# The second block's attention: last turned copy and output scaling on VectorE, scores between the transposes

## The chip, the cores and the metric

The kernel runs on one core of one Trainium2 chip. The metric is the device time of one execution in microseconds (us); the profile is one further execution of the same program, taken by the hardware profiler. TensorE (PE) multiplies matrices and transposes tiles, its weight loads (PEld) run ahead of its matmuls; VectorE (DVE), ScalarE (ACT) and GpSimd (POOL) work elementwise; SyncE (SP) issues DMAs. Each engine runs its own list of instructions in order, and the lists meet at semaphores only.

## What is computed

The reference is a long chain: a first block (latent attention, mLSTM, mixture of experts) and a second block of two layers. The change touches the attention of the second block alone, which is run once in each layer (l = 0 and l = 1). Cut to that:

```python
# k_all, v_all: 256 context tokens and then 1024 latent tokens; 4 query heads of 64, 2 key/value heads
def latent_attention(q, k_all, v_all):          # 1024 queries, 1280 keys
    s = einsum('bqhd,bkhd->bhqk', q, k_all)     # float32 scores, in blocks of 128 queries
    return einsum('bhqk,bkhd->bqhd', softmax(s), v_all)
# layer 0 also attends the 256 context queries to the 256 context keys; layer 1, the last, does not
o_att = silu(z) * attention                     # one of four branches of the layer
```

## The kernel before

The program is a row of phases with a barrier of all engines after each. In each layer of the second block they are: norm, `project_in`, `attention_2`, `fourier`, `project_out`. Nothing of the next phase's engine work begins before `attention_2` has ended; the weights of the later phases are fetched by DMA during it (`prefetch`, early in SyncE's list).

`attention_2` walks a list `items` of tiles, a tile being 128 queries of one head. Long tiles have 1280 keys, short tiles (context queries, layer 0 only) have 256. Layer 0 has, for each of 4 heads, 8 long tiles and then 2 short ones, 40 in all; layer 1 has 4 times 8 long tiles, 32 in all. For tile n the work is:

- `scores(n)`, TensorE: queries times keys into the PSUM tile `at_sc` (two buffers of three banks), with the key split into a high and a low part `kh`, `klo`: six matmuls for 1280 keys, two for 256.
- `maximum(n)`, VectorE: the row maximum, and with it the bias of the exponential.
- `exp(n)`, ScalarE: the exponential into `at_p` (two buffers), with its row sum in `total`; `inv` is the reciprocal, taken on VectorE.
- `turn`, TensorE: the 128x128 pieces of `at_p` are transposed into the PSUM tile `at_tb`, which has two buffers of one bank. The pieces go in groups of four: a long tile has the groups g0 and g1 of four pieces and g2 of two; a short tile has one group of two.
- copy of each turned group from `at_tb` to `at_pT`: on ScalarE (`copy_turned`).
- `output(n)`, TensorE: `at_pT` times `at_v`, 10 matmuls (20 records) for a long tile, written into the free part of the bank in which the last group of tile n+1 lies, right after that group's transposes.
- scaling of the output by `inv` and copy out of PSUM (`copy_output`): on ScalarE, after the copy of that last group.

TensorE's list for tile n: first `scores(n + 2)`, then g0, g1, g2, then `output(n - 1)`. Uses of the two `at_tb` buffers are numbered; `full` says that TensorE has filled a use, `free` that it has been read out. Before the last group, TensorE waits for these:

```python
                            m = first_use[n] - 1
                            pe.wait_ge(free[m % 2], m // 2 + 1)
                            if first_use[n] - first_use[n - 1] > 1:
                                pe.wait_ge(free[1 - m % 2], (m - 1) // 2 + 1)
```

that is, all groups of tile n - 1 have been copied; the group itself also needs its own buffer, which g0 of the same tile held. ScalarE's list for tile n: `exp(n + 1)`, copy g0, copy g1, copy g2, scale the output of tile n - 1. VectorE's: `maximum(n + 1)`, reciprocal of tile n.

Once in each call, before head 2, the keys are exchanged (`KEYS_1`): ScalarE makes `kh` anew (`split_high`) when all scores of heads 0 and 1 are done, VectorE then makes `klo`, and only then may `scores` of the first tile of head 2 go. In ScalarE's list this stands ahead of the tile `2 * per_head - 2`, behind everything of the tile before it.

In the profile the line of a matmul made by the helper `accumulate` is L145 (scores and outputs alike; the tile names tell them apart), that of a transpose L3091, the copies are L3173, the scaled output L3168, the exponential L3151, the maximum L3210 and L3213.

Of the kernel before, what the change touches and what calls it, by code (L numbers as in the profile page):

```python
# [11 lines left out]
ALU = mybir.AluOpType  # L12
ACT = mybir.ActivationFunctionType
# [3 lines left out]
P = 128  # L17
# [31 lines left out]
H2, KVH, HD = 4, 2, 64  # L49
# [2937 lines left out]
def attention_2(nc, g, l, last, prefetch):  # L2987
# [5 lines left out]
    with Phase(nc, f"at{l}") as ph:  # L2993
# [4 lines left out]
        p = ph.sb("p", [P, 2, N_ALL])  # L2998
        pT = ph.sb("pT", [P, 2, NT, P])
# [5 lines left out]
        full = [ph.sem(f"full{b}") for b in range(2)]  # L3005
        free = [ph.sem(f"free{b}") for b in range(2)]
        names = ("scored", "maxed", "bias_ready", "exped", "inv_ready", "raw_in", "high", "low", "y_done",
                 "cleared", "y_turned", "pool_high", "pool_low", "first_in")
        scored, maxed, bias_ready, exped, inv_ready, raw_in, high, low, y_done, cleared, y_turned, pool_high, pool_low, first_in = (
            ph.sem(n) for n in names)  # L3010

        items = []
# [36 lines left out]
        def half(h):  # L3049

            return slice((h % 2) * HD, (h % 2) * HD + HD)

        with nc.Block() as block:
# [30 lines left out]
            @block.tensor  # L3084
            def _(pe):
                def turn(n, srcs, more=None):
                    b = n % 2
                    if n >= 2:
                        pe.wait_ge(free[b], n // 2)
                    for k, src in enumerate(srcs):  # L3090
                        mm = pe.transpose(tb[:, b, k * P:(k + 1) * P], src, g.ident[:])  # L3091
                    if more is not None:
                        mm = output(b, more)
                    mm.then_inc(full[b], 1)

                def output(b, n):
                    h, _, keys = items[n]
                    return accumulate(nc, tb[:, b, 2 * P:2 * P + HD], [
                        (pT[:, n % 2, k, :], v[:, k, (h // 2) * HD:(h // 2 + 1) * HD]) for k in range(keys // P)])

                def scores(n):
                    h, q0, keys = items[n]
                    if n == 0:
                        pe.wait_ge(cleared, 1)
                    if n % per_head == 0:
                        pe.wait_ge(*need[h])
                        if h == 2:
                            split_done(pe, KEYS_1)
                    if n >= 2:
                        pe.wait_ge(exped, n - 1)  # L3110
                    for c0 in range(0, keys, BANK):
                        cols = slice(c0, min(c0 + BANK, keys))
                        mm = accumulate(nc, sc[:, n % 2, c0 // BANK, 0:cols.stop - c0], [
                            (q[:, h % 2, q0:q0 + P], kh[:, cols]), (q[:, h % 2, q0:q0 + P], klo[:, cols])])
                    mm.then_inc(scored, 1)

                for c, (t0, tn) in enumerate(groups(N_ALL)):
                    turn(c, [g.parts[:, V_AT, (t0 + k) * P:(t0 + k + 1) * P] for k in range(tn)])
                scores(0)
                scores(1)  # L3120
                for n, (h, q0, keys) in enumerate(items):
                    if n + 2 < len(items):
                        scores(n + 2)
                    pe.wait_ge(exped, n + 1)
                    gs = groups(keys)
                    for c, (t0, tn) in enumerate(gs):

                        more = n - 1 if c == len(gs) - 1 and n else None
                        if more is not None:
                            m = first_use[n] - 1  # L3130
# [3 lines that stand above are left out]
                        turn(first_use[n] + c, [p[:, n % 2, (t0 + k) * P:(t0 + k + 1) * P] for k in range(tn)], more)  # L3134
                end = first_use[-1]
                for m in (end - 1, end - 2):
                    pe.wait_ge(free[m % 2], m // 2 + 1)
                output(end % 2, len(items) - 1).then_inc(full[end % 2], 1)
                pe.wait_ge(y_done, 1)
                for n, (t, c0, cn) in enumerate(ends):  # L3140
                    for c in range(cn):
                        mm = pe.transpose(sc[:, n // 3, n % 3, c * P:(c + 1) * P],
                                          y[t][:, c0 + c, :], g.ident[:])
                    mm.then_inc(y_turned, 1)

            @block.scalar
            def _(act):
                def exp(n):
                    h, q0, keys = items[n]
                    act.wait_ge(bias_ready, n + 1)  # L3150
                    act.activation(p[:, n % 2, 0:keys], sc[:, n % 2].rearrange("p b n -> p (b n)")[:, 0:keys], ACT.Exp,  # L3151
                                   bias=st[:, n % 2, 1:2], scale=g.rq[:, q0 // P, h:h + 1],
                                   accum_out=total[:, n % 4:n % 4 + 1]).then_inc(exped, 1)

                def split_high(i):
                    what, h = loads[i]
                    loaded(act, i)
                    if i == KEYS_1:
                        act.wait_ge(scored, 2 * per_head)
                    if what == "k":  # L3160
                        act.activation(kh[:], raw[:], ACT.Copy).then_inc(high, 1)
                    else:
                        act.activation(q[:, h % 2, lo:], source(i)[:, lo:], ACT.Copy).then_inc(high, 1)

                def copy_output(b, n):
                    h, q0, _ = items[n]
                    act.wait_ge(inv_ready, n + 1)
                    return act.activation(y[h // 2][:, q0 // P, half(h)], tb[:, b, 2 * P:2 * P + HD], ACT.Copy,  # L3168
                                          scale=inv[:, n % 4:n % 4 + 1])

                def copy_turned(m, dst, w, output_of=None):
                    act.wait_ge(full[m % 2], m // 2 + 1)
                    ins = act.activation(dst, tb[:, m % 2, 0:w], ACT.Copy)  # L3173
                    if output_of is not None:
                        ins = copy_output(m % 2, output_of)
                    ins.then_inc(free[m % 2], 1)

                split_high(KEYS_0)
                split_high(QUERIES_0)
                for c, (t0, tn) in enumerate(groups(N_ALL)):  # L3180
                    copy_turned(c, v[:, t0:t0 + tn, :].rearrange("p t d -> p (t d)"), tn * P)
                exp(0)
                for n in range(len(items)):
                    if n in splits_at:
                        split_high(splits_at[n])
                    if n + 1 < len(items):
                        exp(n + 1)
                    gs = groups(items[n][2])
                    for c, (t0, tn) in enumerate(gs):
                        copy_turned(first_use[n] + c, pT[:, n % 2, t0:t0 + tn, :].rearrange("p t d -> p (t d)"), tn * P,  # L3190
                                    n - 1 if c == len(gs) - 1 and n else None)
                end = first_use[-1]
                act.wait_ge(full[end % 2], end // 2 + 1)
                copy_output(end % 2, len(items) - 1).then_inc(y_done, 1)

            @block.vector
            def _(dve):
# [9 lines left out]
                def maximum(n):  # L3207
# [5 lines left out]
                    dve.tensor_scalar(st[:, n % 2, 1:2], st[:, n % 2, 0:1], g.rq[:, q0 // P, h:h + 1], -1.0,  # L3213
                                      ALU.mult, ALU.mult).then_inc(bias_ready, 1)

                split_low(KEYS_0)
                split_low(QUERIES_0)
                maximum(0)
                for n, (h, q0, keys) in enumerate(items):
                    if n in splits_at:  # L3220
                        split_low(splits_at[n])
                    if n + 1 < len(items):
                        maximum(n + 1)
                    dve.wait_ge(exped, n + 1)
                    dve.reciprocal(inv[:, n % 4:n % 4 + 1], total[:, n % 4:n % 4 + 1]).then_inc(inv_ready, 1)
                for n, (t, c0, cn) in enumerate(ends):
                    dve.wait_ge(y_turned, n + 1)
                    cols = slice(c0 * P, (c0 + cn) * P)
                    dve.tensor_tensor(g.o[2 + t][:, cols], sc[:, n // 3, n % 3, 0:cn * P], g.parts[:, ZA_AT + t, cols], ALU.mult)
# [457 lines left out]
```

## Time and profile before

| | |
|---|---|
| runs | 3838.62 us median of 3 (3837.56 to 3839.77) |
| the profiled execution | 3839.44 us, its span 3837.7 us |
| busy over the span | TensorE 3337.1 us (87%), VectorE 1843.9 (48%), ScalarE 1473.2 (38%), GpSimd 709.8 (18%) |
| attention of layer 0 | about 2818 to 3012 us of the span; TensorE busy 164.7 of 194.0 |
| attention of layer 1 | about 3512 to 3699 us of the span; TensorE busy 161.9 of 187.0 |

The two attentions are a tenth of the time. Shares of busy time over the whole span say little about them; they have to be read from their own stretches, and there from the waits of the engine that is busiest.

### The profile page before, as it was taken

Reading aid. Unit: us, or ns where it says so; the run is one execution under the profiler, and the core shown is the slowest. Engines: PE = TensorE matmul, PEld = TensorE weight load, DVE = VectorE, ACT = ScalarE, POOL = GpSimd, SP = SyncE. Lnnn points to the kernel's source line nnn. Section 1 sums busy time; section 2 is a strip of 40 time slices with the busy share of each in tenths; the row PEclk is TensorE's granted clock in tenths of the full one; section 3 lists DMA queues with packets and bytes.
Section 4 is the critical chain, followed back from the end, with each engine's and each line's share of the span. In section 5 each row is a group of like instructions: output and inputs, shape, how many; then the busy total and the mean of one; then the engine's idle time right before and its main releaser. Section 6 shows DMA issues by size and latency. Waiting matters only on the chain. (4 is left out here: it accounts for less than half of the span.)

```text
span 3837.7 us, 42815 instructions
## 1 busy us (share of the span) xinstructions
PE 3337.1 (87%) x17015; PEld 2690.6 (70%) x17015; DVE 1843.9 (48%) x2343; ACT 1473.2 (38%) x2230; POOL 709.8 (18%) x463
## 2 busy tenths in 40 slices
PE   6999998999999499794999996399978895998889
PEld 3777775777777377573878875288867684886767
DVE  3366874334333354646888885614323433252333
ACT  4222322333434144433777774421145304113531
POOL 2100100000110144202555543400000002000000
PEclk7999999999999699896999998599999997999989
DMA  5335554001010121327999995311030023113002
GB/s 185 110 102 180 187 185 134 24 24 31 24 41 1 57 108 54 138 94 293 382 381 380 389 380 184 132 48 37 27 110 8 23 88 107 53 46 100 13 11 89
DMA packets 235384, 475.87 MB, mean 124 GB/s; under 512 B 25539, under 2 KB 120644, under 8 KB 235188
## 3 DMA queue, kind: packets, MB, share of 16 engines
q1 hardware_dynamic: 219600, 415.26, 31.2%
q0 software_dynamic: 15264, 57.70, 4.5%
q8 instruction: 140, 2.29, 0.2%
q14 instruction: 56, 0.46, 0.0%
q10 hardware_dynamic: 324, 0.15, 0.0%
HBM read 410.50 MB, written 55.22 MB: 121 GB/s over the span
## 5 line engine op out<-in xcount | busy, mean ns | idle before, releaser
L2371 DVE TENSOR_TENSOR exp_wl<-wts_raw,exp_wh 128x2048 fp32r<-128x2048 f32 x144 | 393.9, 2770 | 105.9 <-ACT exp_wh L2331 105.9
L2331 ACT ACTIVATE exp_wh<-wts_raw 128x2048 fp32r<-128x2048 f32 x192 | 368.0, 1919 | 196.0 <-PE exp_gate L2260 64.1
L2704 PE MATMUL pr_ps<-l_h_high,pr_wh 128*128 128x512 f32 (+1 forms) x896 | 335.4, 374 | 18.9 <-DVE pr_wl L2843 18.9
L2705 PE MATMUL pr_ps<-l_h_low,pr_wh 128*128 128x512 f32 (+1 forms) x896 | 330.5, 369 | 0.0
L2706 PE MATMUL pr_ps<-l_h_high,pr_wl 128*128 128x512 f32 (+1 forms) x896 | 329.8, 368 | 0.0
L729 PE MATMUL in_ps<-iw_h_high,in_wh 128*128 128x512 f32 (+1 forms) x696 | 274.9, 395 | 13.9 <-DVE in_wl L907 13.9
L2229 POOL TENSOR_TENSOR exp_wl<-wts_raw,exp_wh 128x2048 fp32r<-128x2048 f32 x48 | 228.9, 4770 | 263.5 <-ACT exp_wh L2331 263.5
L730 PE MATMUL in_ps<-iw_h_low,in_wh 128*128 128x512 f32 (+1 forms) x696 | 264.6, 380 | 0.0
L731 PE MATMUL in_ps<-iw_h_high,in_wl 128*128 128x512 f32 (+1 forms) x696 | 264.1, 379 | 0.0
L2843 DVE TENSOR_TENSOR pr_wl<-pw_raw,pr_wh 128x512 fp32r<-128x512 f32 x88 | 60.1, 691 | 357.8 <-ACT pr_wh L2765 356.0
L2704 PEld LDWEIGHTS pr_ps<-l_h_high,pr_wh 128*128 128x128 f32 x896 | 170.2, 190 | 50.5 <-DVE pr_wl L2843 19.7
L1305 DVE TENSOR_REDUCE att_st<-att_sc 128x1 f32<-128x1280 f32 x64 | 95.4, 1491 | 213.6 <-PE att_sc L145 213.4
L3210 DVE TENSOR_REDUCE at_st<-at_sc 128x1 f32<-128x1280 f32 (+1 forms) x72 | 98.8, 1372 | 200.9 <-PE at_sc L145 200.9
L2705 PEld LDWEIGHTS pr_ps<-l_h_low,pr_wh 128*128 128x128 f32 x896 | 170.1, 190 | 30.2 <-issue 2.4
L2706 PEld LDWEIGHTS pr_ps<-l_h_high,pr_wl 128*128 128x128 f32 x896 | 169.8, 190 | 28.3
L729 PEld LDWEIGHTS in_ps<-iw_h_high,in_wh 128*128 128x128 f32 x696 | 133.2, 191 | 50.3 <-DVE in_wl L907 14.3
L2765 ACT ACTIVATE pr_wh<-pw_raw 128x512 fp32r<-128x512 f32 x88 | 54.9, 630 | 275.0 <-PE pr_ps L2706 268.5
L145 PE MATMUL at_tb<-at_v,at_pT 128*128 128x64 f32 x1312 | 157.4, 275 | 1.4 <-ACT at_y L3168 1.4
L145 PEld LDWEIGHTS at_tb<-at_v,at_pT 128*128 128x128 f32 x1312 | 155.2, 195 | 1.6 <-ACT at_y L3168 1.6
L3173 ACT ACTIVATE at_pT<-at_tb 128x512 f32<-128x512 f32 (+1 forms) x200 | 97.6, 526 | 152.4 <-PE at_tb L145 149.4
L145 PE MATMUL att_tb<-att_pT,att_v 128*128 128x128 f32 x1280 | 153.5, 275 | 0.7 <-ACT att_pT L1272 0.7
L730 PEld LDWEIGHTS in_ps<-iw_h_low,in_wh 128*128 128x128 f32 x696 | 133.1, 191 | 28.9 <-issue 5.1
(505 smaller groups left out, 7559.4 us busy)
## 6 DMA issues: line engine op xcount, KB each, us to landing
wts_raw<-in_w_e_gate SPq DMA_DIRECT2D x64, 1024.0 KB, 9.8
wts_raw<-in_w_e_up SPq DMA_DIRECT2D x64, 1024.0 KB, 9.3
wts_raw<-in_w_e_down SPq DMA_DIRECT2D x64, 1024.0 KB, 7.7
in_mw<-in_w_mod SPq DMA_DIRECT2D x80, 512.0 KB, 4.5
pw_raw<-in_w_in SPq DMA_DIRECT2D x88, 256.0 KB, 2.9
iw_raw<-in_w_in SPq DMA_DIRECT2D x74, 256.0 KB, 4.7
mod_w<-in_w_mod SPq DMA_DIRECT2D x4, 2048.0 KB, 11.9
wo_w<-in_w_out SPq DMA_DIRECT2D x2, 4096.0 KB
```

Source lines behind the costliest of these rows:

```text
L145: mm = nc.tensor.matmul(out, lhsT, rhs, start=n == 0, stop=n == last)
L729: nc.tensor.matmul(out, wh[:, slot, k, :], hi, start=h == 0 and k == 0, stop=False)
L730: nc.tensor.matmul(out, wh[:, slot, k, :], lw, start=False, stop=False)
L731: mm = nc.tensor.matmul(out, wl[:, slot, k, :], hi, start=False, stop=h == 1 and k == KH - 1)
L2229: pool.tensor_tensor(wl[:, POOL_SLOT], raw[:, m % RAW_RING], wh[:, POOL_SLOT].bitcast(F32), ALU.subtract).then_inc(low_pool, 1)
L2331: act.activation(wh[:, m % RING], raw[:, m % RAW_RING], ACT.Copy).then_inc(high, 1)
L2371: dve.tensor_tensor(wl[:, m % RING], raw[:, m % RAW_RING], wh[:, m % RING].bitcast(F32), ALU.subtract).then_inc(low, 1)
L2704: nc.tensor.matmul(out, wh[:, slot, k, :], hi, start=h == 0 and k == 0, stop=False)
L2705: nc.tensor.matmul(out, wh[:, slot, k, :], lw, start=False, stop=False)
L2706: mm = nc.tensor.matmul(out, wl[:, slot, k, :], hi, start=False, stop=h == 1 and k == KH - 1)
L3173: ins = act.activation(dst, tb[:, m % 2, 0:w], ACT.Copy)
L3210: dve.tensor_reduce(st[:, n % 2, 0:1], sc[:, n % 2].rearrange("p b n -> p (b n)")[:, 0:keys], AX.X, ALU.max).then_inc(maxed, 1)
```

## The change

VectorE takes over the copy of each tile's last turned group and the scaling of the output (`copy_last`, `copy_output`), one step later in its own list; ScalarE keeps the exponentials and the copies of the other groups. Since ScalarE's list no longer meets TensorE's at the end of a tile, `exp(n)`, which overwrites `p`, gets a wait of its own: a new semaphore `p_turned` counts the tiles whose last group has been transposed. And on TensorE `scores(n + 2)` moves from ahead of tile n's transposes to between its g0 and g1 (in a short tile, which has one group, it stays where it was).

```diff
@@ TensorE
                     for k, src in enumerate(srcs):
                         mm = pe.transpose(tb[:, b, k * P:(k + 1) * P], src, g.ident[:])
                     if more is not None:
+                        mm.then_inc(p_turned, 1)
                         mm = output(b, more)
                     mm.then_inc(full[b], 1)
...
                 for n, (h, q0, keys) in enumerate(items):
-                    if n + 2 < len(items):
-                        scores(n + 2)
                     pe.wait_ge(exped, n + 1)
                     gs = groups(keys)
                     for c, (t0, tn) in enumerate(gs):
 
+                        if c == min(1, len(gs) - 1) and n + 2 < len(items):
+                            scores(n + 2)
                         more = n - 1 if c == len(gs) - 1 and n else None
@@ ScalarE
                 def exp(n):
                     h, q0, keys = items[n]
                     act.wait_ge(bias_ready, n + 1)
+                    if n == 2:
+                        m = first_use[1] - 1
+                        act.wait_ge(full[m % 2], m // 2 + 1)
+                    if n > 2:
+                        act.wait_ge(p_turned, n - 2)
...
-                    gs = groups(items[n][2])
-                    for c, (t0, tn) in enumerate(gs):
-                        copy_turned(first_use[n] + c, pT[:, n % 2, t0:t0 + tn, :].rearrange("p t d -> p (t d)"), tn * P,
-                                    n - 1 if c == len(gs) - 1 and n else None)
-                end = first_use[-1]
-                act.wait_ge(full[end % 2], end // 2 + 1)
-                copy_output(end % 2, len(items) - 1).then_inc(y_done, 1)
+                    for c, (t0, tn) in enumerate(groups(items[n][2])[:-1]):
+                        copy_turned(first_use[n] + c, pT[:, n % 2, t0:t0 + tn, :].rearrange("p t d -> p (t d)"), tn * P)
@@ VectorE
+                def copy_output(b, n):
+                    h, q0, _ = items[n]
+                    dve.wait_ge(inv_ready, n + 1)
+                    return dve.tensor_scalar(y[h // 2][:, q0 // P, half(h)], tb[:, b, 2 * P:2 * P + HD], inv[:, n % 4:n % 4 + 1],
+                                             None, ALU.mult)
+
+                def copy_last(n):
+                    t0, tn = groups(items[n][2])[-1]
+                    m = first_use[n + 1] - 1
+                    dve.wait_ge(full[m % 2], m // 2 + 1)
+                    ins = dve.tensor_copy(pT[:, n % 2, t0:t0 + tn, :].rearrange("p t d -> p (t d)"), tb[:, m % 2, 0:tn * P])
+                    if n:
+                        ins = copy_output(m % 2, n - 1)
+                    ins.then_inc(free[m % 2], 1)
...
                     dve.wait_ge(exped, n + 1)
                     dve.reciprocal(inv[:, n % 4:n % 4 + 1], total[:, n % 4:n % 4 + 1]).then_inc(inv_ready, 1)
+                    if n:
+                        copy_last(n - 1)
+                copy_last(len(items) - 1)
+                end = first_use[-1]
+                dve.wait_ge(full[end % 2], end // 2 + 1)
+                copy_output(end % 2, len(items) - 1).then_inc(y_done, 1)
```

TensorE's list in layer 0's attention, one tile and the beginning of the next, among the long tiles of head 0 (`at_sc` the scores, `at_tb` transposes of `at_p` and the output). Before:

```order
L3091 MATMUL at_tb<-g_ident,at_p 128x128 x10
L145 MATMUL at_tb<-at_v,at_pT 128x64 x10
L145 MATMUL at_sc<-at_kh,at_q 128x512
L145 MATMUL at_sc<-at_klo,at_q 128x512
L145 MATMUL at_sc<-at_kh,at_q 128x512
L145 MATMUL at_sc<-at_klo,at_q 128x512
L145 MATMUL at_sc<-at_kh,at_q 128x256
L145 MATMUL at_sc<-at_klo,at_q 128x256
```

and with the change, at the same place:

```order
L3091 MATMUL at_tb<-g_ident,at_p 128x128 x6
L145 MATMUL at_tb<-at_v,at_pT 128x64 x10
L3091 MATMUL at_tb<-g_ident,at_p 128x128 x4
L145 MATMUL at_sc<-at_kh,at_q 128x512
L145 MATMUL at_sc<-at_klo,at_q 128x512
L145 MATMUL at_sc<-at_kh,at_q 128x512
L145 MATMUL at_sc<-at_klo,at_q 128x512
L145 MATMUL at_sc<-at_kh,at_q 128x256
L145 MATMUL at_sc<-at_klo,at_q 128x256
```

Four of a tile's ten transposes now go ahead of the scores; nothing is added or taken away. ScalarE's list at the same tiles, before:

```order
L3173 ACTIVATE at_pT<-at_tb 128x512 x2
L3173 ACTIVATE at_pT<-at_tb 128x256
L3168 ACTIVATE l_parts<-at_tb,at_inv 128x64
L3151 ACTIVATE at_p,at_total<-at_sc,at_st,l_rq 128x1280
```

and VectorE's list for one tile with the change, where the last two rows are new:

```order
L3202 TENSOR_REDUCE at_st<-at_sc 128x1
L3205 TENSOR_SCALAR at_st<-at_st,l_rq 128x1
L3232 RECIPROCAL at_inv<-at_total 128x1
L3218 COPY at_pT<-at_tb 128x256
L3211 TENSOR_SCALAR l_parts<-at_tb,at_inv 128x64
```

ScalarE's second and third rows have become VectorE's fourth and fifth, and stand there behind the maximum of tile n + 1 and the reciprocal of tile n.

## Rows read from the trace of the kernel before

**Rows 1.** Waits of the weight loads (PEld), attention of layer 0: total, times, longest

```profile
PEld at_tb L3091 <- issue: 28.8, 33, 1.5
PEld at_sc L145 <- issue: 4.3, 2, 3.5
PEld at_sc L145 <- ACT at_p L3151: 2.7, 4, 1.5
PEld at_tb L145 <- ACT at_y L3168: 0.8, 1, 0.8
...
PEld at_sc L3142 <- ACT at_y L3168: 0.5, 1, 0.5
```

**Rows 2.** The same, attention of layer 1

```profile
PEld at_tb L3091 <- issue: 23.5, 31, 1.5
...
PEld at_sc L145 <- issue: 4.1, 2, 3.5
PEld at_sc L145 <- ACT at_p L3151: 2.4, 1, 2.4
...
PEld at_tb L3091 <- ACT at_y L3168: 0.7, 2, 0.5
...
PEld at_tb L3091 <- ACT at_pT L3173: 0.4, 1, 0.4
```

**Rows 3.** Timeline, one long tile, layer 0: start, duration, instruction [idle before, releaser]

```profile
2843.61 1.43 ACT L3151 ACTIVATE at_p<-at_sc,at_st,l_rq 128x1280 f32<-128x1280 f32 x1
...
2844.05 0.90 PEld L3091 LDWEIGHTS at_tb<-g_ident,at_p 128*128 128x128 f32 x8
...
2845.00 1.09 ACT L3173 ACTIVATE at_pT<-at_tb 128x512 f32<-128x512 f32 x2
2845.72 0.20 PEld L3091 LDWEIGHTS at_tb<-g_ident,at_p 128*128 128x128 f32 x2 [0.77 <-issue]
...
2848.38 0.39 ACT L3173 ACTIVATE at_pT<-at_tb 128x256 f32<-128x256 f32 x1 [2.29 <-PE at_tb L145]
...
2848.86 1.42 ACT L3151 ACTIVATE at_p<-at_sc,at_st,l_rq 128x1280 f32<-128x1280 f32 x1
```

**Rows 4.** Timeline, a tile without a stall of TensorE, and the way to an exponential

```profile
2864.19 0.24 PEld L3091 LDWEIGHTS at_tb<-g_ident,at_p 128*128 128x128 f32 x2
...
2866.63 0.19 PEld L145 LDWEIGHTS at_sc<-at_kh,at_q 128*128 128x128 f32 x1
...
2867.80 0.24 PEld L3091 LDWEIGHTS at_tb<-g_ident,at_p 128*128 128x128 f32 x2
...
2868.10 1.49 DVE L3210 TENSOR_REDUCE at_st<-at_sc 128x1 f32<-128x1280 f32 x1 [1.80 <-PE at_sc L145]
...
2869.62 0.22 DVE L3213 TENSOR_SCALAR at_st<-at_st,l_rq 128x1 f32<-128x1 f32 x1
...
2869.88 1.42 ACT L3151 ACTIVATE at_p<-at_sc,at_st,l_rq 128x1280 f32<-128x1280 f32 x1 [0.53 <-DVE at_st L3213]
```

**Rows 5.** VectorE's nearest operations out of PSUM: count | busy us, mean ns | idle before

```profile
L2551 DVE TENSOR_SCALAR l_parts<-fin_tp,fin_gain,g_mod 128x128 f32<-128x128 f32 x40 | 13.6, 402 | 6.8 <-PE fin_tp L2594 6.8
...
L2887 DVE TENSOR_SCALAR l_parts<-pr_ex 128x256 f32<-128x256 f32 x2 | 0.8, 424 | 0.3 <-PE pr_ex L145 0.2
```

**Rows 6.** Timeline, the exchange of keys in layer 1

```profile
3592.57 1.27 ACT L3161 ACTIVATE at_kh<-at_raw 128x1280 fp32r<-128x1280 f32 x1
...
3595.45 0.76 PE L145 MATMUL at_sc<-at_kh,at_q 128*128 128x512 f32 x1 [3.40 <-issue]
...
3602.86 0.47 PE L145 MATMUL at_sc<-at_kh,at_q 128*128 128x512 f32 x1
```

**Rows 7.** Busy time by stretch, layer 1: PE, PEld, DVE, ACT, POOL, PEclk, DMA share, GB/s

```profile
3575.00:3580.00 5.00, 4.43 (x36) 4.05 (x35) 1.77 (x3) 2.96 (x6) 0.00 (x0) 1.00 0.00 0
...
3595.00:3600.00 5.00, 4.55 (x16) 3.89 (x17) 3.81 (x7) 2.44 (x4) 0.00 (x0) 0.50 0.52 108
...
3685.00:3690.00 5.00, 5.00 (x33) 4.57 (x32) 0.00 (x0) 1.78 (x4) 0.00 (x0) 0.68 0.01 3
```

More of the change, by code:

```diff
@@ L3007, in attention_2 @@
         names = ("scored", "maxed", "bias_ready", "exped", "inv_ready", "raw_in", "high", "low", "y_done",
-                 "cleared", "y_turned", "pool_high", "pool_low", "first_in")
-        scored, maxed, bias_ready, exped, inv_ready, raw_in, high, low, y_done, cleared, y_turned, pool_high, pool_low, first_in = (
+                 "cleared", "y_turned", "pool_high", "pool_low", "first_in", "p_turned")
+        scored, maxed, bias_ready, exped, inv_ready, raw_in, high, low, y_done, cleared, y_turned, pool_high, pool_low, first_in, p_turned = (
             ph.sem(n) for n in names)
@@ L3163, in split_high, with copy_turned @@
                         act.activation(q[:, h % 2, lo:], source(i)[:, lo:], ACT.Copy).then_inc(high, 1)
[L3165 to L3171, printed above, removed]
+                def copy_turned(m, dst, w):
                     act.wait_ge(full[m % 2], m // 2 + 1)
[L3173 to L3176, printed above, removed]
+                    act.activation(dst, tb[:, m % 2, 0:w], ACT.Copy).then_inc(free[m % 2], 1)
                 split_high(KEYS_0)
```

## The prediction

> **What bounds the kernel now.** The change lies in two phases of their own, so I read those alone and ask who sets a tile's length. TensorE does: it is busy for 85 to 87% of them (the table above). I take its weight loads (PEld) as its clock, since their start times run without overlap. In layer 0 they wait 28.8 + 4.3 + 2.7 us, and 3.3 in five small rows (0.8 to 0.5) [rows 1], 39.1 in all; in layer 1 23.5 + 4.1 + 2.4, and 2.5 in four small rows (0.8, as the largest small one of layer 0, to 0.4) [rows 2], 32.5. Together 71.6 us: more than this change can't take from the waits.
>
> Where the largest of them comes from is seen in one tile [rows 3]. TensorE loads for its first eight transposes from 2844.05 to 2844.95. The two turned groups could be copied then, but ScalarE began `exp(n + 1)` only at 2843.61 and copies from 2845.00; g2 needs g0's buffer, so TensorE's next load stands 0.77 us. Why is the exponential late? Its scores were long done. ScalarE stood 2.29 us, until TensorE had ended `output(n - 1)`, then copied g2 (2848.38) and scaled the output, and only then could the next exponential start (2848.86). So it is a ring: output, copy of g2 and scaling, exponential, copy of g0, g2's transposes. A tile takes 2848.86 - 2843.61 = 5.25 us.
>
> A short tile without such a stall gives TensorE's own work: from 2864.19 to 2867.80, that is 3.61 us for two transposes, an output and scores [rows 4], of which the scores are 1.17. With 0.90 for the eight transposes [rows 3] a long tile is 4.51 us of work. The stall costs 5.25 - 4.51 = 0.74.
>
> The second wait is 3.5 us at the exchange of keys, once in each layer [rows 1, 2]: ScalarE turns to `kh` only after scaling an output (3592.57), VectorE's half follows, and TensorE goes on at 3595.45 after 3.40 us of nothing [rows 6]. Behind it the granted clock is 0.50 in its stretch against 1.00 in the ordinary tiles [rows 7], which is the 1.2 GHz level: that tile takes 3602.86 - 3595.45 = 7.41 us instead of 4.51.
>
> **The change, part by part.** Nothing is added on TensorE but a signal. I set t = 0 at the first load of tile n's g0 and walk one long tile in the new order: g0 to 0.45, `scores(n + 2)` to 1.62, g1 to 2.07, g2 to 2.30, output to 4.5. A signal of TensorE reaches its waiter 0.30 after the last load here (2867.80 to 2868.10) [rows 4]; for transposes and outputs I take 0.2 to 0.25.
>
> *VectorE's pair.* The trace has no such copy. A read of the same 128x256 from PSUM took 0.42 [rows 5]. For the scaling, 128x64, the bounds are nothing and the 0.40 of a 128x128 with two scalars [rows 5]; taking the slope of one column per ns between these two rows it comes nearer 0.3, and I use 0.28. The pair is then 0.70 (at most 0.42 + 0.40, or, were the copy as dear as both, 1.1). On ScalarE both took 0.48 until it was free again [rows 3]. The Trainium skill (VectorE: DVE Perf Modes, The TRN2 errata) gives 120 cycles plus one a column at 0.96 GHz for VectorE out of PSUM. That would be 0.39 and 0.19, 0.58 for the pair, and the sum below would be 1 to 2 us larger; it also says that ScalarE sits closer to PSUM, which no row here shows for these shapes.
>
> VectorE waits for `full` of tile n - 1, which comes at t = 0.25, and is done by 1.0. First to need it is g1 (its bank), at 1.62: 0.6 us of cover, so the pair may cost 1.3 before a long tile feels it. Behind the waiting copy in VectorE's list stands `maximum(n + 2)`, whose scores are there at 1.9: not delayed.
>
> *ScalarE.* Maximum 1.49, 1.52 to the next step, 0.26 from there to the exponential (2869.62 to 2869.88) [rows 4]. `exp(n + 1)` so starts at 1.62 - 4.53 + 0.30 + 1.52 + 0.26 = -0.83; its copies follow 1.39 later (2843.61 to 2845.00) [rows 3], at 0.56, and g0 is full at 0.64. Its copy of about 0.6 ends near 1.3; g2 wants it at 2.07. The new wait for `p_turned` (t = 2.5 of the tile before) lies ahead of the exponential's bias (3.7 on the same scale) and costs nothing. So the ring is open and a long tile is TensorE's own 4.5 us. Both halves of the change are needed for it. In the old order g2 would follow g0's end by 0.45, g1's transposes alone, while signal and copy take 0.9: with ScalarE free 0.45 of stall would stay. The scores put 1.17 more between them. By the walk described next, the copies alone gain 27 us, the new order alone loses 1, and both gain 46.
>
> *What is left.* I walked all 40 and 32 tiles with these durations. The same walk in the old order gives 71.2 us of waits (the rows 71.6). In the new order it leaves, in layer 0: the wait for the first exponential 2.5 and for the last output 0.6, as before; 1.4 until the ring is running; 0.3 in tiles 7 and 8 of each head, where short scores cover less of VectorE's pair (2.5); 0.57 and 0.87 in the first long tile after the short ones, three times (4.3); 1.0 before each of the last outputs, for VectorE's pair, which was 0.7 on ScalarE (3.0); 0.2 and at the exchange of keys 1.1. Together 15.6. In layer 1: 2.5, 0.6, 1.4, exchange 0.6 + 1.3 + 0.9, last tiles 2.1: 9.4. The gain is 71.2 - 25.0 = 46.2; I take 46.
>
> *The exchange of keys* is in this sum. ScalarE's list reaches `kh` right after copying g1, 2.8 us into the tile before, not behind its output: done 4.1, VectorE's half (as long as a maximum) 5.6, while the new order wants the scores at 4.5 + 0.45. About 0.6 of the 3.4 stays. With no idle of 3.4 us in front, the slow clock behind it should stay away: 7.41 - 4.51 = 2.9 us in layer 1 [rows 6, 4, 3]; in layer 0 a short tile stands there, half the work, for which I estimate 1.5. Together 4.4.
>
> Sum: 46 + 4.4 = 50.4 us. From the profiled execution, 3839.44, that gives 3789.0; it was 0.8 above the median, so I predict 3788 us. No DMA hides it: SyncE's fetches for later phases are issued early in the phase, and its end is a barrier.
>
> **The rivals.** *One, the forecast (80 in 100)*: 40 to 62 us less. The near end is the pair at 1.1 (the walk gives 17.5 + 22.4 + 4.4 = 44) and some cost of going from transposes to scores and back, which no row has; at 0.1 a tile 6 us more is lost. The far end has half of the waits that the walk leaves, (25.0 - 6.2) / 2 = 9 us more, and 3 for less of the slow clock in the last tiles, which by [rows 7] come at 0.68.
>
> *Two, half (10 in 100)*: TensorE pays for the interleaving 0.2 to 0.4 us a tile, 64 tiles, 13 to 26 us: 3801 to 3814. The trace shows no gap when output turns to scores or scores to transposes, one after another in every tile [rows 4]; that speaks against it.
>
> *Three, the clock (4 in 100)*: TensorE's clock falls in stretches without long scores. In the last tiles, which have none, the granted clock was 0.68 with TensorE wholly busy [rows 7]. If the same came at the short tiles of each head, at 2.9 us each time as behind the keys, four times cost 12 and the first keys' gain goes: about 3802. Against it: there are short scores between, and the mix over a tile is what it was while idle time shrinks. The Trainium skill (TensorE: Matmul & The Clock Gate, Part 4) says that transposes do not count as activity for the clock. Were that what decides, the new order, which parts scores and outputs by transposes on both sides, could lose the full clock in every long tile; the trace has 1.00 in tiles with ten transposes in a row [rows 7].
>
> *Four, slower (3 in 100)*: VectorE's pair becomes the ring. Past 1.3 us each microsecond of it lengthens the long tile by as much; at 1.3 + 0.74 = 2.05 nothing is gained, and at 3 us 64 tiles lose 0.95 each, 61 us, less the 4 of the clock: about 3895. The rows put the pair at a third of the point where it decides.
>
> *Five, nothing (3 in 100)*: something else of the phase (an exponential waiting for `p_turned`, VectorE's list in disorder) takes the place of the stall, within 0.2% of before, about 8 us, which is what a measurement of this kernel can tell.
>
> **How the numbers follow.** The likeliest case gives 3788. The range takes it whole and the nearer part of the second and third: 3776 to 3804. Faster by over 0.2%: 0.94; within: 0.03; slower: 0.03.
>
> **What would show it.** In the changed profile: long tiles 4.5 us apart; no wait of g2 for ScalarE's copy; VectorE's COPY 128x256 near 0.42 and its TENSOR_SCALAR 128x64 near 0.28; ScalarE waiting for `at_tb` transposes and no longer for outputs; a wait of under 1.5 us at the keys and a clock of 1.00 behind it; the phases, by the stretches of the table, near 169 and 160 us long. I am wrong if TensorE waits for VectorE in ordinary long tiles, if its own work in a tile is over 4.7 us, or if the clock falls in new places.

## The result and the profile after

The changed kernel took 3782.93 us (median of 4 runs, 3778.48 to 3788.15) against 3839.19 before: ratio 0.9845, 95% interval 0.9823 to 0.9867, 56 us less. The forecast was 3788, with 3776 to 3804. On another chip it took 3786.61 (ratio 0.9856, 0.9835 to 0.9877). Its profiled execution took 3785.64 us, its span 3783.6.

To see where the time went I cut every span at the same points: in either layer the first scores and the first of the transposes that close the attention's phase (L3142 before, L3143 after, L3144 where reads were added). The starts are read from TensorE's timeline of each run, in us. The experiments, which are told below, stand in the same table; `rest` is what follows layer 1's phase, and `long tile` is the distance of one long tile from the next:

| run | before layer 0's scores | phase, layer 0 | between | phase, layer 1 | rest | long tile |
|---|---|---|---|---|---|---|
| before | 2818.7 | 192.6 | 502.4 | 183.1 | 140.9 | 5.25 |
| changed | 2815.9 | 166.0 | 502.7 | 156.1 | 142.9 | 4.44 |
| changed, again | 2819.3 | 165.8 | 500.0 | 156.3 | 142.5 | 4.44 |
| e1_order | 2817.1 | 195.9 | 502.4 | 187.6 | 139.3 | 5.25 |
| e2_copies | 2817.6 | 178.4 | 501.1 | 167.4 | 141.3 | 5.02 |
| e3_extra1 | 2818.6 | 170.7 | 500.4 | 159.7 | 140.4 | 4.44 |
| e4_extra3 | 2821.4 | 191.5 | 501.2 | 167.9 | 141.1 | 4.76 |
| e5_keys | 2816.3 | 164.9 | 500.9 | 151.6 | 140.4 | 4.44 |
| e6_both | 2819.2 | 163.6 | 501.5 | 151.0 | 141.2 | 4.44 |
| e7_extra6 | 2818.0 | 243.7 | 500.6 | 203.6 | 142.7 | 5.75 |

The two phases give 26.6 + 27.0 = 53.6 us. The stretches that the change doesn't touch differ by up to 5.5 us from run to run, so the phases are the better measure of a part.

One long tile of the changed kernel in its timeline, the counterpart of [rows 3]:

```profile
2842.36 1.42 ACT L3157 ACTIVATE at_p<-at_sc,at_st,l_rq 128x1280 f32<-128x1280 f32 x1 [0.74 <-DVE at_st L3205]
2843.11 0.48 PEld L3091 LDWEIGHTS at_tb<-g_ident,at_p 128*128 128x128 f32 x4
...
2843.42 0.42 DVE L3218 COPY at_pT<-at_tb 128x256 f32<-128x256 f32 x1 [1.03 <-PE at_tb L145]
...
2843.77 0.27 DVE L3211 TENSOR_SCALAR l_parts<-at_tb,at_inv 128x64 f32<-128x64 f32 x1
2843.87 0.60 ACT L3173 ACTIVATE at_pT<-at_tb 128x512 f32<-128x512 f32 x1
...
2844.73 0.68 PEld L3091 LDWEIGHTS at_tb<-g_ident,at_p 128*128 128x128 f32 x6
2845.03 1.49 DVE L3202 TENSOR_REDUCE at_st<-at_sc 128x1 f32<-128x1280 f32 x1 [0.99 <-PE at_sc L145]
2845.38 2.31 PEld L145 LDWEIGHTS at_tb<-at_v,at_pT 128*128 128x128 f32 x20
...
2846.80 1.42 ACT L3157 ACTIVATE at_p<-at_sc,at_st,l_rq 128x1280 f32<-128x1280 f32 x1 [0.74 <-DVE at_st L3205]
```

In this tile no weight load has an idle time in brackets any more. The exponential waits for VectorE's bias, not for an output's end; VectorE's copy begins 0.31 us after g0's first load. ScalarE and VectorE both stand idle for a time, and TensorE alone sets the length, 2846.80 - 2842.36 = 4.44 us. What VectorE's new operations cost, over all tiles, by shape (the other 36 scalings write `l_parts` and take 275 ns):

```profile
L3218 DVE COPY at_pT<-at_tb 128x256 f32<-128x256 f32 x72 | 30.4, 423 | 84.2 <-PE at_tb L145 84.2
...
L3211 DVE TENSOR_SCALAR at_y<-at_tb,at_inv 128x64 f32<-128x64 f32 x36 | 9.9, 276 | 3.9 <-PE at_tb L145 3.9
```

The waits of the weight loads in layer 0, as [rows 1]; the eight rows, of which six stand here, add up to 14.4 us where they were 39.1:

```profile
PEld at_tb L3091 <- issue: 5.9, 7, 1.1
PEld at_sc L145 <- issue: 2.0, 2, 1.2
PEld at_tb L3091 <- DVE l_parts L3211: 1.7, 6, 0.4
PEld at_tb L3091 <- ACT at_p L3157: 1.5, 1, 1.5
PEld at_tb L3091 <- DVE at_y L3211: 1.3, 5, 0.4
PEld at_tb L145 <- DVE at_y L3211: 0.8, 1, 0.8
```

In layer 1 (as [rows 2], without the wait for the turned values, which lies ahead of the first scores) they are 8.8 where they were 32.5.

At the exchange of keys in layer 1, as [rows 6], three waits are left, and behind them the output and g0 take nearly double. (These are the matmuls' waits. A weight load's is some 0.2 longer: 0.78, 1.00 and 1.09 at the same places.)

```profile
3553.12 0.47 PE L145 MATMUL at_sc<-at_kh,at_q 128*128 128x512 f32 x1 [0.57 <-issue]
...
3555.31 0.66 PE L3091 MATMUL at_tb<-g_ident,at_p 128*128 128x128 f32 x4 [0.80 <-DVE l_parts L3211]
3556.85 0.41 PE L3091 MATMUL at_tb<-g_ident,at_p 128*128 128x128 f32 x2 [0.88 <-ACT at_pT L3173]
3557.09 3.86 PE L145 MATMUL at_tb<-at_v,at_pT 128*128 128x64 f32 x20
3560.74 1.06 PE L3091 MATMUL at_tb<-g_ident,at_p 128*128 128x128 f32 x4
```

The stretches of time, as [rows 7] (the sixth figure behind the length of a stretch is the granted clock): full in the ordinary tiles, fallen behind the keys, and fallen again only as the phase ends at 3640.7:

```profile
3505.00:3510.00 5.00, 5.00 (x44) 4.83 (x42) 2.95 (x6) 2.91 (x5) 0.00 (x0) 1.00 1.04 407
3555.00:3560.00 5.00, 3.81 (x23) 3.60 (x23) 1.94 (x5) 3.70 (x6) 2.64 (x2) 0.76 0.34 66
3560.00:3565.00 5.00, 5.00 (x24) 4.61 (x24) 1.64 (x3) 0.86 (x2) 0.75 (x1) 0.55 0.00 0
3635.00:3640.00 5.00, 4.29 (x37) 4.16 (x36) 0.61 (x2) 0.07 (x1) 0.00 (x0) 0.96 0.01 3
3640.00:3645.00 5.00, 4.03 (x18) 3.44 (x17) 2.92 (x5) 0.00 (x0) 0.00 (x0) 0.50 0.00 0
```

### The profile page after: what moved, and what is told of

It reads as the page before. It is cut to its first block and busy times, and to the rows that moved or that the text cites. A ratio compares the mean times of both kernels' runs of the same rounds, so it can differ in the third digit from the quotient of the medians.

```text
span 3783.6 us, 42884 instructions
## 1 busy us (share of the span) xinstructions
PE 3322.4 (88%) x17015; PEld 2687.9 (71%) x17015; DVE 1886.7 (50%) x2487; ACT 1448.9 (38%) x2086; POOL 709.8 (19%) x463
## 5 line engine op out<-in xcount | busy, mean ns | idle before, releaser
L731 PEld LDWEIGHTS in_ps<-iw_h_high,in_wl 128*128 128x128 f32 x696 | 132.4, 190 | 25.1
L145 PEld LDWEIGHTS att_tb<-att_pT,att_v 128*128 128x128 f32 x1280 | 148.0, 192 | 0.9 <-issue 0.9
```

Source lines behind the costliest of these rows:

```text
L145: mm = nc.tensor.matmul(out, lhsT, rhs, start=n == 0, stop=n == last)
L731: mm = nc.tensor.matmul(out, wl[:, slot, k, :], hi, start=False, stop=h == 1 and k == KH - 1)
```

## The experiments

**The two halves apart.** First the new order alone, on the kernel before:

```diff
                 for n, (h, q0, keys) in enumerate(items):
-                    if n + 2 < len(items):
-                        scores(n + 2)
                     pe.wait_ge(exped, n + 1)
...
+                        if c == min(1, len(gs) - 1) and n + 2 < len(items):
+                            scores(n + 2)
```

> The kernel before with one part of the change: scores(n + 2) between g0 and g1, all copies still on ScalarE. Theory (the ring through ScalarE bounds a tile; the order gives cover only once ScalarE is free): within 3 us of before, 3836 to 3840 us; long tiles stay near 5.2 us, and TensorE still waits in each for ScalarE, only at another group. Rival A (the gain is the new order's, which gives g0's copy 1.17 us more): 20 us or more off, 3820 or less, tiles near 4.8.

Measured: 3845.93 us against 3837.22 of the kernel before, ratio 1.0023 (1.0013 to 1.0033). One tile in the timeline:

```profile
3531.50 1.43 ACT L3151 ACTIVATE at_p<-at_sc,at_st,l_rq 128x1280 f32<-128x1280 f32 x1
...
3533.64 0.41 PE L3091 MATMUL at_tb<-g_ident,at_p 128*128 128x128 f32 x2 [0.61 <-ACT at_pT L3173]
...
3536.27 0.38 ACT L3173 ACTIVATE at_pT<-at_tb 128x256 f32<-128x256 f32 x1 [2.28 <-PE at_tb L145]
```

Rival A is out: a long tile stays at 5.25 us, g2 still waits for ScalarE and ScalarE still 2.28 us for the output. The ring runs through ScalarE, and moving scores within TensorE's list doesn't touch it. But the kernel is 9 us slower, not within 3 as expected, and the phases are 3.3 and 4.5 us longer. The weight loads' waits grow by 3 us only (74.5 for 71.6). What grows is the time at the clock's 1.2 GHz level: summed over the two phases from granted clocks of 5 us stretches it is 45 us, before it was 28. Most of that is behind the keys. In layer 1:

```profile
3595.00:3600.00 5.00, 2.65 (x8) 2.30 (x9) 3.31 (x5) 1.80 (x2) 0.00 (x0) 0.62 0.34 69
3600.00:3605.00 5.00, 4.60 (x23) 4.23 (x22) 1.64 (x3) 1.42 (x4) 3.10 (x2) 0.50 0.19 39
3605.00:3610.00 5.00, 5.00 (x23) 4.61 (x22) 1.08 (x1) 2.71 (x6) 0.28 (x1) 0.51 0.00 0
```

The wait there is no longer than before (2.96 us against 3.40), but the clock stays at its 1.2 GHz level for some 14 us where it was 7. In layer 0, behind a wait of 3.56 us, it is 10 us where it was 3. Why it comes back later I can't say; it is seen, not explained.

The copies alone: the changed kernel with the order of before (the same lines the other way round).

> The changed kernel with scores(n + 2) back ahead of g0: copies of g2 and output scaling on VectorE alone. Theory: 30 us off (walk: 16 in layer 0, 14 in layer 1), 3807 to 3812 us; long tiles near 4.9 us, each with a stall of g2 of about 0.4 for g0's copy by ScalarE. Rival A: near before, 3830 or more. Rival B (the copies are all of it, the order nothing): as the changed kernel, 3780 to 3788, tiles 4.44.

Measured: 3808.55 us, ratio 0.9927 (0.9911 to 0.9944), 29 us off:

```profile
3528.34 0.41 PE L3091 MATMUL at_tb<-g_ident,at_p 128*128 128x128 f32 x2 [0.34 <-ACT at_pT L3173]
...
3531.98 1.03 PE L3091 MATMUL at_tb<-g_ident,at_p 128*128 128x128 f32 x8
...
3532.62 1.08 ACT L3173 ACTIVATE at_pT<-at_tb 128x512 f32<-128x512 f32 x2 [2.17 <-PE at_tb L3091]
```

ScalarE is free now: it waits 2.17 us for g0, and still g2 is late by the 0.34 that signal and copy take beyond g1's transposes. So Rival B (the order is worth nothing) is out too: it is worth nothing alone and 0.58 us a tile once the copies have moved (5.02 to 4.44). The phases lose 14.2 and 15.6 us, 29.8, where the walk said 30. The split is another: 5.25 to 5.02 is only 0.23 for each of 64 tiles, 15 us. All waits of the weight loads fall from 71.6 to 49, so some 7 us more come from the heads' ends and the keys. The other 8 are the clock's: it stands at 1.2 GHz for 9 us of the two phases, all at their beginnings, where before it was 28. In layer 1 TensorE still waits 0.53, 0.36 and 0.88 us at the keys, and the clock stays full over them:

```profile
3570.00:3575.00 5.00, 3.60 (x24) 2.84 (x23) 4.91 (x7) 1.80 (x4) 0.00 (x0) 1.00 0.48 96
3575.00:3580.00 5.00, 4.64 (x36) 4.29 (x36) 1.86 (x6) 2.57 (x5) 3.42 (x2) 1.00 0.05 12
```

**How much cover VectorE's pair has.** One more read of the last group, then three, then six, ahead of the copy:

```diff
                     dve.wait_ge(full[m % 2], m // 2 + 1)
+                    for k in range(1):      # 3, 6
+                        dve.tensor_reduce(idle[:, n % 8, k:k + 1], tb[:, m % 2, 0:tn * P], AX.X, ALU.max)
                     ins = dve.tensor_copy(pT[:, n % 2, t0:t0 + tn, :]...
```

> The changed kernel with one more VectorE read of the last turned group ahead of its copy (a row maximum of 128x256 out of PSUM into a column that nobody reads, 0.42 us by its row): pair from 0.70 to 1.12. Theory (the pair has 0.6 us of cover in a long tile, less in short ones): long tiles stay at 4.44 to 4.50; 7 us more than the changed kernel (6 in layer 0, 1 in layer 1), about 3788 to 3791. Rival C (VectorE is idle half of the time, so it absorbs it wholly): no more than 1 us. Rival D (the pair has no cover): 0.42 for each of 72 tiles, 30 us.

> The same with three more reads: pair 1.97. Theory: past its cover each microsecond of the pair lengthens a long tile: tiles near 5.1 us, the gain gone: 50 to 60 us more than the changed kernel, 3830 to 3845, layer 0 worse (34) than layer 1 (22). Rival C: under 10 us more, since VectorE would still be busy less than 80% of a tile. Rival D: 72 times 1.27, 91 us more, 3870 or above.

> As e4_extra3 with six more VectorE reads for each tile. By e4_extra3's rows a read takes 0.33 us of VectorE's time and the pair 0.62, so the pair with its six is 2.58. Theory (a cover of 1.28, past it one for one): long tiles 4.44 + 2.58 - 1.28 = 5.74 us, half a microsecond longer than before the change; phases 30 and 29 us longer than e4_extra3's, the kernel slower than before by 40 to 50 us, 3875 to 3890. Rival (only the part past VectorE's own idle time counts): VectorE's list for a tile is 1.52 + 0.13 + 0.15 + 2.58 = 4.4 us, so tiles stay at 4.5 to 4.8.

Measured: 3793.77 us (ratio 0.9886, 0.987 to 0.9903), 3824.82 (0.9966, 0.9954 to 0.9979) and 3911.4 (1.0186, 1.0167 to 1.0206). In e7_extra6's timeline:

```profile
3594.56 2.08 DVE L3220 TENSOR_REDUCE at_idle<-at_tb 128x1 f32<-128x256 f32 x6 [1.43 <-PE at_tb L145]
...
3596.56 0.42 DVE L3221 COPY at_pT<-at_tb 128x256 f32<-128x256 f32 x1
3596.89 0.28 DVE L3212 TENSOR_SCALAR l_parts<-at_tb,at_inv 128x64 f32<-128x64 f32 x1
3597.08 1.48 DVE L3203 TENSOR_REDUCE at_st<-at_sc 128x1 f32<-128x1280 f32 x1
3597.22 0.64 PEld L3092 LDWEIGHTS at_tb<-g_ident,at_p 128*128 128x128 f32 x6 [1.29 <-DVE l_parts L3212]
```

Six reads take 2.00 us from start to start, 0.33 each, and not the 0.42 that a row gives as one's duration: in the trace each begins before the one ahead of it has ended. The pair by itself is 2843.77 - 2843.42 + 0.27 = 0.62. So with one, three and six reads it is 0.95, 1.60 and 2.62, and the long tiles take 4.44, 4.76 and 5.75. From three reads to six the pair grows by 1.0 and the tile by 1.0: past its cover it counts one for one. The cover (how much the pair may take before a long tile feels it) is 1.60 - (4.76 - 4.44) = 1.28, and the tile would be back at 5.25 with a pair of 2.09. Both are what the prediction's fourth rival gave (1.3 and 2.05). Rival C (VectorE's idle half absorbs it) is out, and D (no cover) too. Where I was off is in the expectation of e4_extra3, in which I added 0.42 a read: 3830 to 3845, and it is 3825.

Short tiles have less cover, as expected: with one read, which no long tile feels, layer 0's phase is 4.7 us longer than the changed kernel's (I expected 6), and its weight loads wait 3.6 us more. Layer 1 has no short tiles and is 3.6 us longer all the same, where I expected 1; its waits grow by 1 us, but it spends 20 us at the 1.2 GHz level and not 13. That brings the kernel to 3794, 3 us above the range expected.

With six reads the long tile comes as expected (5.75 for 5.74), but the kernel is 21 us slower than the expected 3875 to 3890. Layer 0's phase is 52 us longer than with three, not 30, and layer 1's 36, not 29. In layer 0 TensorE's clock falls at the short tiles of every head and is low for 73 us of the phase, against 21 with three reads:

```profile
2915.00:2920.00 5.00, 3.33 (x22) 3.33 (x23) 2.23 (x9) 1.20 (x4) 0.00 (x0) 0.81 0.00 0
2920.00:2925.00 5.00, 3.58 (x18) 3.29 (x18) 2.60 (x8) 0.61 (x2) 0.00 (x0) 0.50 0.00 0
2925.00:2930.00 5.00, 5.00 (x24) 4.90 (x23) 2.53 (x6) 2.39 (x4) 0.00 (x0) 0.50 0.16 33
```

That is the place that the third rival named, but not clearly its mechanism, which was a lack of long scores while TensorE is wholly busy: here TensorE stands for 2.02 us just ahead of the fall.

```profile
2916.67 0.88 PE L3092 MATMUL at_tb<-g_ident,at_p 128*128 128x128 f32 x6 [2.02 <-DVE l_parts L3212]
```

The same holds for the 0.68 on which that rival rested [rows 7]: just before that stretch stands, in the kernel before, a wait of 1.32 us that I hadn't looked at.

```profile
3684.40 0.41 PE L3091 MATMUL at_tb<-g_ident,at_p 128*128 128x128 f32 x2 [1.32 <-ACT at_pT L3173]
```

No run tells the missing scores from the waits. The change as it is has its clock at 1.00 in the short tiles of the first three heads, and it falls only 1.1 us before layer 0's phase ends; a pair four times as dear sets it off at every head.

**The clock behind the keys, and what is left.** The next kernel, e5_keys, is the changed one with the exchange moved in two lists: ScalarE makes the new high keys between its copies of g0 and g1 of the tile before, and VectorE makes the low ones behind the next maximum:

```diff
@@ ScalarE
-                    if n in splits_at:
-                        split_high(splits_at[n])
...
                     for c, (t0, tn) in enumerate(groups(items[n][2])[:-1]):
+                        if c == 1 and n + 1 in splits_at:
+                            split_high(splits_at[n + 1])
@@ VectorE
-                    if n in splits_at:
-                        split_low(splits_at[n])
                     if n + 1 < len(items):
                         maximum(n + 1)
+                    if n in splits_at:
+                        split_low(splits_at[n])
```

> The changed kernel with the exchange of keys earlier in two lists: ScalarE makes the new high keys between the copies of g0 and g1 of the tile before, VectorE makes the low ones behind the next maximum, not ahead of it. Theory (the waits of 0.57, 0.80 and 0.88 us there, 2.25 in a row of 4 us, are what lets TensorE's clock fall behind them): layer 1's waits there fall to 0.5 or less and the clock stays at 1.00, 2 + 3 us; layer 0 gains 1: phases near 165 and 151 us, 6 us off the changed kernel. Rival E (the clock falls there for another reason, its work or the time since it last fell): layer 1's granted clock falls at the same place all the same, 3 us off in all.

Measured: 3779.21 us (3775.92 to 3780.1) beside 3786.61 (3779.56 to 3789.4) of the changed kernel on the same chip, for which I expected

> The changed kernel again, as the base for e5_keys and e6_both on the same chip: 3780 to 3787 us, phases 166.0 and 156.1 us.

The phases are 164.9 and 151.6 us where I expected 165 and 151. In layer 1 TensorE never waits at the keys, and it keeps its clock:

```profile
3550.00:3555.00 5.00, 5.00 (x39) 4.75 (x39) 2.91 (x8) 3.03 (x6) 0.81 (x1) 1.00 0.52 105
3555.00:3560.00 5.00, 5.00 (x40) 4.72 (x39) 2.39 (x5) 3.04 (x5) 2.59 (x2) 1.00 0.00 0
3560.00:3565.00 5.00, 5.00 (x43) 4.83 (x42) 2.60 (x6) 2.70 (x4) 0.00 (x0) 1.00 0.01 3
```

Of layer 1's 4.7 us less, 2.25 are the waits at the keys (0.57, 0.80 and 0.88); the rest is the clock that doesn't fall there. Rival E is out: with TensorE's list unchanged and the waits gone, the clock stays. How much waiting makes it fall isn't shown; e2_copies bore 0.53, 0.36 and 0.88 at the same place.

Last, the same with one more thing: in the first long tile after short ones ScalarE copies g0 before the next exponential.

> The kernel of e5_keys, and in the first long tile after short ones ScalarE copies g0 ahead of the exponential of the next tile. Theory: the three waits of 0.88 us of layer 0's g2 for ScalarE's copy of g0 go (the exponential comes 0.6 later and is wanted 3 us later): 2.6 us off layer 0 beside e5_keys, phase near 162.5; 8 to 9 us off the changed kernel in all. Rival: the later exponential only moves the wait to the next tile, 0 to 1 us off.

Measured: 3778.54 us (3774.91 to 3780.68), ratio 0.9839 (0.9822 to 0.9855) like e5_keys: not told apart from it by time. The phase of layer 0 is 1.3 us shorter, where I expected 2.6. Each of the three waits of 0.88 has become one of

```profile
2867.58 0.63 PE L3091 MATMUL at_tb<-g_ident,at_p 128*128 128x128 f32 x4 [0.27 <-ACT at_pT L3173]
```

one tile later, which is between what I expected (none) and its rival. Both versions beat the changed kernel by 7 to 8 us in their medians, and by 5.6 and 7.5 in the two phases together.

## Why the prediction was right

- *The ring* (output, copy and scaling on ScalarE, exponential, copy of g0): shown. e1_order leaves it and keeps 5.25 us a tile, e2_copies opens it and g2's wait shrinks to 0.34.
- *Both halves are needed*: shown. Alone the copies gave 29.8 us of the phases (I wrote 27), the order lost 7.8 (I wrote 1), together 53.6. My walk had no clock in it. By the weight loads' waits alone the copies gave 22, the order lost 3 and both gave 48; most of the difference is the clock's each time, so the nearness of 27 to 29.8 is partly luck.
- *A long tile is TensorE's own work*: 4.44 us, where I had 4.51. About half of that difference is my sum, not the change: without its wait a long tile took 5.25 - 0.77 = 4.48 before [rows 3]. An output that is followed by transposes takes 2.18 us (2840.93 to 2843.11 in the timeline's loads), where it takes 2.23 in front of scores (3580.52 to 3582.75 in e2_copies), and the ten transposes in two parts take some of that back. The 4.44 also rules out the second rival, a cost of interleaving.
- *VectorE's pair*: 0.423 and 0.276 us by the rows, where I had 0.42 and 0.28; occupied for 0.62. The estimates from the Trainium skill's figures (VectorE: DVE Perf Modes, The TRN2 errata), 0.39 and 0.19, were low for both, more so for the small one.
- *The waits left*: 14.4 + 8.8 = 23.2 us, where the walk had 15.6 + 9.4 = 25.0. Most single ones, here those of the matmuls, came out near the walk: 1.12 at layer 0's keys (1.1), 0.88 three times in the first long tiles (0.87), 0.57, 0.80 and 0.88 at layer 1's keys (0.6, 1.3, 0.9). Ahead of each of the three 0.88 stands one of 0.21, where I had 0.57.
- *The slow clock* was the weak step. I wrote that with no idle of 3.4 us in front it should stay away. In layer 0 it did. In layer 1 it fell behind waits of 0.57, 0.80 and 0.88 and cost about 3 us: the output there took 3.65 instead of 2.18, g0 and scores 3.00 instead of 1.61. Of that row's 2.9 us nothing was won, and a sign that I had named for the forecast, a clock of 1.00 behind the keys, failed there; e5_keys wins it.

The term as a whole came out all the same, from other places. At its 1.2 GHz level the clock stood for 8.3 and 19.3 us of the two phases before and stands for 5.6 and 12.8 now, 9 us less. At the keys 7 such us cost 3, so I estimate 4 us for these, where I had 4.4. Besides the 3.4 low us at layer 0's keys, what went are low stretches of layer 1 that my sum left out, in its first tiles and in its last (the last ones I had at the far end of the range only), against 2.4 more at its very beginning. Before, they were:

```profile
3520.00:3525.00 5.00, 4.82 (x22) 4.03 (x22) 1.78 (x3) 3.18 (x6) 0.00 (x0) 0.70 0.85 270
3690.00:3695.00 5.00, 4.32 (x32) 4.18 (x31) 0.00 (x0) 0.59 (x2) 0.00 (x0) 0.84 0.00 0
3695.00:3700.00 5.00, 4.59 (x22) 4.41 (x22) 1.74 (x3) 0.31 (x1) 0.00 (x0) 0.50 0.00 0
```

Now the clock falls 1.2 us before layer 1's phase ends and is still low in the next phase, where `rest` is 2 us longer.

The sum, then: 48.4 us of waits and about 4 of clock, 52.4 of the 53.6; the last microsecond, as far as the estimate of the clock carries, is TensorE's own work. The forecast's 46 + 4.4 was 3 us short of it in the phases, some 2 of them in the waits. The mechanism of the large term was right. That the clock's term is right in size is luck: its larger half didn't come, and terms that weren't in the sum filled its place.

## What to carry to other kernels

When the busiest engine stalls a little in every round, follow the late partner back until the chain closes. Here the late exponential was late because its engine also emptied the other end of the pipeline; giving that end to an idle engine broke the ring, and only then did reordering the busy engine pay. Ask of a moved operation how much cover it has, not how idle its new engine is: VectorE was busy for half the time, and yet had 1.3 us to spare, past which each microsecond cost one. And where waits get shorter, the clock may move with them: read its low time in each stretch beside the waits, or a right total hides two wrong parts.

## What was unexpected about the hardware

- TensorE's granted clock fell to the 1.2 GHz level behind three waits of 0.57, 0.80 and 0.88 us within 4 us, none of them long (in both profiles of the changed kernel), and stayed at 1.00 behind a single one of 1.12 in layer 0 and behind 0.53, 0.36 and 0.88 in e2_copies. With those waits gone it stayed at 1.00.
- The new order by itself kept the clock low for 14 us behind a wait of 2.96, where it had been 7 behind 3.40, and for 10 where it had been 3 in layer 0. The cause stays open.
- A VectorE read of 128x256 out of PSUM has a duration of 0.42 us in its row, but six in a row take 0.33 each.
- The four runs of the changed kernel spread over 10 us, and go with the mean granted clock: 3778.5 and 3780.2 at 0.935, 3785.6 and 3788.2 at 0.932.
